# One unit forward: diagonals and first decays of the mLSTM heads, two value products behind a turn, and GpSimd's waits

## The chip, the cores and the metric

The kernel runs on one core of one Trainium2 chip. The metric is the device time of one execution in microseconds; lower is better. Everything is float32 at the interface. Large products are computed as three matmuls on operands split in a rounded part (fp32r, names ending in `_hi`) and a remainder (`_lo`).

## The reference

Two transformer blocks follow each other on a sequence of 512 tokens of width 1024. The first has a convolution branch, a sparse attention, a cross attention and a feed-forward layer. The change lies in the token mixer of the second block, which has two parts beside each other:

- an mLSTM of 4 heads (key width 64, value width 128): scores of queries and keys, weighted by a causal decay exp(gate of the key minus a running maximum m of the query), times the values; each row is divided by a norm, passed through an RMS norm, and gated;
- a latent causal attention (MLA) of 8 heads (q.k of width 96, value width 64) in query blocks of 128.

```
D = b[..., :, None] - b[..., None, :] + ig[..., None, :]
Dw = jnp.exp(D - m_comb[..., None])
s = jnp.einsum('bhcid,bhcjd->bhcij', qc, kc) * Dw
num = ... s @ v ...;  h = num / jnp.maximum(jnp.abs(den), jnp.exp(-m_comb))[..., None]
h_ml = rmsnorm(h_ml, ...) * jax.nn.sigmoid(o_ml)          # 4 heads
h_mla = causal_block_attention(q, k, kv[..., MLA_NOPE:])  # 8 heads, blocks of 128 queries
return jnp.concatenate([h_ml, h_mla], axis=-1) @ w_out
```

The kernel computes an mLSTM head without chunks: 4 key blocks jb of 128 keys, each against all queries from its own block on.

## The kernel before, in words

The program is one in-order list of instructions for each engine, written out by hand; semaphores join them. In the stretch that the change touches, every engine runs a loop over **units** n = 0 to 31, one for each of 8 latent heads x 4 query blocks, and then five more units (32 to 36). Unit n on TensorE (PE) is: the latent scores of unit n + 2, then a hook with the work of other stages (`beside`: steps of three 512-column matmuls of the mLSTM values and output gates, `BESIDE` says how many in each unit; `ml_turn`: the transposes of a finished mLSTM head; `ml_score`), then `ml_values` (the values of one key block), and at some units `latent_values(h)`, 10 matmuls (20 records) of a latent head whose probabilities went through HBM to be turned (`l_turned`).

mLSTM head h starts at unit 3 + 7h; its step st is n - 3 - 7h. By step:

- st -1, ACT (L2059 to L2064): DMA that broadcasts the head's row of m from HBM to all partitions (`mrow`);
- st 1, VectorE (DVE, L3114 to L3121): the four **diagonals** `negm_diag`, 128x128 each, from `mrow` and a mask. They wait for `mrow` and for the decays of the head before;
- st 2 to 5, ACT (L2066 to L2076): `decay` of key block 0 to 3, an exp of the diagonal block and one of the columns right of it. The one of block 0 is the **first decay**;
- st 3 to 6, PE: score of key block jb into the one bank `ps[3]`; DVE then multiplies it with the decay to `sT` (L3093), which frees the bank for the next score;
- st 4 to 7, PE: values of the block; the first of a head waits for `ml_gated`, that is for `hml` (L3137) of the head before, which takes its turned rows from the bank;
- st 7 and 8: squares on ACT (L2080), `ml_var` on DVE (L3110), the **root** on ACT (L2085). The root is a Sqrt, so ACT loads a table before it and another one before the next exp;
- st 9, DVE: `ml_rows` (L3124 to L3127), the scaled rows; st 11 (10 for the last head): `ml_turn` on PE (L1367), `hml` on DVE; st 12: `mix_hi` on ACT (L2088).

DVE's unit n is: reciprocal of the row sums n (`rowinv`, L3192), mask of unit n + 2 (L3186), `hml` where due, `sT`, the transpose of the probabilities of unit n - 1 (`l_parts`, L3199), `latent_lo`, then `ml_rest` with the diagonals or `ml_rows`. ACT's unit n is: `latent_hi`, probabilities n scaled by `rowinv` (L2135), exp of unit n + 2 (L2129), then its hook: weight casts (`cast_at`), the step of every head, output gates.

`latent_values(h)` needs the landed `l_turned`, and `latent_lo(h - 1)` on DVE, behind `latent_hi(h - 1)` on ACT, which empty its bank. SP issues, in an order written out by hand, the stores of `l_parts`, the loads of `l_turned` and the weight chunks `w_raw`. GpSimd (POOL) computes weight remainders `w_lo` (L655), `mix_lo` of the mLSTM heads (L726) and 16 products on the residual (L716, L719); waits place them.

Of the kernel before, what the change touches and what calls it, by code (L numbers as in the profile page):

```python
# [31 lines left out]
TB = T // P  # L32
# [10 lines left out]
ML_HEADS = 4  # L43
# [178 lines left out]
GATES_AT = 1  # L222
LATE_CASTS = 17


def turned_at(h):
    return 10 + (h < ML_HEADS - 1)


# [11 lines left out]
def program(nc, stream, xT, memT, cols_in, consts_in, pos_in, out):  # L241
    with ExitStack() as ctx:
# [406 lines left out]
        def _(pool):  # L649
# [72 lines left out]
            def ml_lo(h):  # L722
                pool.wait_ge(sems["ml_hi"], h + 1)
                if h == 1:
# [5 lines left out]
                              26: (14, 15)}  # L730
            def behind_diagonals(heads):
                pool.wait_ge(sems["ml_diag"], TB * heads)

            remainder(CH["OM"], CH["OM"] % RING)
            behind_diagonals(2)
            remainder(CH["OM"] + 1, (CH["OM"] + 1) % RING)
            for unit in (15, 16):
                second_residual(unit, residual_steps[unit])
            pool.wait_ge(sems["qk_silu"], 6)
            for unit in (17, 18):  # L740
                second_residual(unit, residual_steps[unit])
            behind_diagonals(3)
            remainder(CH["OM"] + 2, (CH["OM"] + 2) % RING)
            ml_lo(0)
            remainder(CH["WO"], 0)
            remainder(CH["WO"] + 1, 1)
            for unit in (23, 24, 25, 26):
                second_residual(unit, residual_steps[unit])
            behind_diagonals(4)
            ml_lo(1)  # L750
            remainder(CH["WO"] + 2, 2)
            ml_lo(2)
            pool.wait_ge(sems["ml_var"], ML_HEADS)
            remainder(CH["WO"] + 3, 3)
# [38 lines left out]
        def _(pe):  # L793
# [626 lines left out]
            for n in range(4 * MLA_HEADS):  # L1420
                if n + 2 < 4 * MLA_HEADS:
                    latent_scores(n + 2)
                turned = n == ML_START + ML_EVERY + turned_at(1)
                ml_hook(n)
                if not turned:
                    ml_values(n)
                if n % 4 == 1 and n >= 9:
                    latent_values(n // 4 - 2)
                if turned:
                    ml_values(n)  # L1430
                ml_turns(n)
# [163 lines left out]
        def _(act):  # L1595
# [461 lines left out]
            def ml_step(h, st):  # L2057
                if st == -1:
# [5 lines left out]
                    act.dma_start(mrow[:, :], m_rows[h:h + 1, :].to_broadcast([P, T])).then_inc(sems["ml_mrow"], 16)  # L2064
                if 2 <= st < 2 + TB:
                    jb = st - 2  # L2066
                    u = 4 * h + jb
                    act.wait_ge(sems["ml_diag"], TB * (h + 1))
                    if u >= 2:
                        act.wait_ge(sems["ml_sT"], u - 1)  # L2070
                    g = gcols[:, 0, jb, h:h + 1]
                    m = A.activation(decay[:, u % 2, 0:P], negm_diag[:, jb, :], ACT.Exp, bias=g)
                    if jb < TB - 1:
                        m = A.activation(decay[:, u % 2, P:T - jb * P], mrow[:, (jb + 1) * P:T], ACT.Exp,
                                         bias=g, scale=-1.0)
                    m.then_inc(sems["ml_decay"], 1)  # L2076
# [16 lines left out]
            def ml_hook(n):  # L2093
# [6 lines left out]
                if n in cast_at and n < LATE_CASTS:  # L2100
                    round_to(cast_at[n])
                for h in range(ML_HEADS):
                    ml_step(h, n - ML_START - ML_EVERY * h)
# [44 lines left out]
            for n in range(4 * MLA_HEADS):  # L2148
                if n % 4 == 2 and n >= 10:
                    latent_hi(n // 4 - 2)  # L2150
                latent_scaled(n)
# [135 lines left out]
        def _(dve):  # L2287
# [825 lines left out]
            def ml_step(h, st):  # L3113
                if st == 1:  # L3114
                    dve.wait_ge(sems["ml_mrow"], 16 * (h + 1))
# [102 lines left out]
            for n in range(4 * MLA_HEADS):  # L3218
# [5 lines left out]
                if n >= 1:  # L3224
                    latent_turn(n - 1)
                if n % 4 == 2 and n >= 10:
                    latent_lo(n // 4 - 2)
                ml_rest(n)
# [370 lines left out]
```

## Time and profile before

| | us |
|---|---|
| median of 3 runs | 1511.98 (1511.72 to 1512.5) |
| the profiled execution | 1512.39 |
| its span, first to last instruction | 1510.6 |
| PE busy | 1490.2 (99%) |
| DVE busy | 1128.3 (75%) |
| ACT busy | 751.5 (50%) |
| GpSimd busy | 627.2 (42%) |

The mean granted TensorE clock is 0.999. Shares of busy time are means over the whole program. Matmuls are pipelined: a 512-column fp32r matmul has 0.39 us in the trace, while the next one starts 0.23 us after it. A wait of PE shows in full in the distance from start to start, and only in part as idle time. The stretch of the units lies between about 1020 and 1135 us of the span.

### The profile page before, as it was taken

How to read it: one execution, taken by the hardware profiler on the slowest of the kernel's cores; microseconds unless marked ns; L12 is line 12 of the kernel's file. 1: busy time of each engine (PE TensorE's matmuls, PEld its weight loads, DVE VectorE, ACT ScalarE, POOL GpSimd, SP SyncE). 2: the span in 40 equal slices, each digit the busy share in tenths (PEclk: the TensorE clock that was granted, in tenths of full speed). 3: DMA queues.
4: the chain of work that ended last, by engine and by line, in shares of the span. 5: the costliest groups of instructions: out<-in, count | busy, mean ns of one | idle time of the engine just before them, and what ended most of it. 6: DMA issues, size and time to landing. Idle time of an engine off the chain costs nothing.

```text
span 1510.6 us, 20173 instructions
## 1 busy us (share of the span) xinstructions
PE 1490.2 (99%) x6978; PEld 1230.5 (81%) x6978; DVE 1128.3 (75%) x1872; ACT 751.5 (50%) x1255; POOL 627.2 (42%) x280
## 2 busy tenths in 40 slices
PE   9999999999999999999999999999999999999998
PEld 7888888878888887888888888786778888888887
DVE  5689999897875445776776768789755887777776
ACT  6553333454562345754544345464964745444434
POOL 3455444332334432144444445451544344444451
PEclk9999999999999999999999999999999999999999
DMA  5332333255543323323333123232653433333451
GB/s 212 98 126 98 98 95 95 89 158 156 158 156 98 98 83 112 102 94 98 112 98 107 54 84 98 84 98 88 181 151 106 144 114 92 109 121 114 142 136 56
DMA packets 77026, 170.40 MB, mean 113 GB/s; under 512 B 22660, under 2 KB 39172, under 8 KB 76680
## 3 DMA queue, kind: packets, MB, share of 16 engines
q1 hardware_dynamic: 75920, 165.64, 35.3%
q10 hardware_dynamic: 1016, 3.61, 0.7%
q8 instruction: 51, 0.84, 0.2%
q14 instruction: 39, 0.32, 0.1%
HBM read 154.54 MB, written 14.69 MB: 112 GB/s over the span
## 4 chain that ended last, share of the span: by engine, by line
PE 86%; DVE 4%; ACT 4%; issue 3%; POOL 1%; DMA 1%; SPq 0%; DVEq 0%; ACTq 0%; POOLq 0%
PE bank L795 86%; POOL w_lo L655 1%; DMA w_raw<-in_stream 1%; ACT w_hi L1604 1%; DVE x_sq L2359 0%; ACT l_probs L2129 0%; DVE bias L2441 0%; POOL res L764 0%; ACT l_probs L2135 0%; ACT dn_first L1898 0%; DVE qk_ml L2999 0%; DMA dn_raw<-in_stream 0%; PE bank L1214 0%; DVE res_tok L3420 0%; PE bank L905 0%
## 5 line engine op out<-in xcount | busy, mean ns | idle before, releaser
L655 POOL TENSOR_TENSOR w_lo<-w_raw,w_hi 128x1024 fp32r<-128x1024 f32 x191 | 472.5, 2484 | 519.2 <-ACT w_hi L1604 511.4
L795 PE MATMUL bank<-a_hi,w_hi 128*128 128x512 f32 (+1 forms) x1120 | 444.6, 397 | 1.8 <-DVE a_lo L3283 1.6
L795 PE MATMUL bank<-a_hi,w_lo 128*128 128x512 f32 (+1 forms) x1120 | 431.4, 385 | 0.0
L795 PE MATMUL bank<-a_lo,w_hi 128*128 128x512 f32 (+1 forms) x1120 | 431.2, 385 | 0.0
L1604 ACT CAST w_hi<-w_raw 128x1024 fp32r<-128x1024 f32 x199 | 204.6, 1046 | 174.2 <-DMA w_raw<-in_stream 174.1
L795 PEld LDWEIGHTS bank<-a_hi,w_hi 128*128 128x128 f32 x1120 | 210.5, 188 | 48.6 <-issue 3.9
L795 PEld LDWEIGHTS bank<-a_lo,w_hi 128*128 128x128 f32 x1120 | 210.5, 188 | 45.3 <-issue 3.4
L795 PEld LDWEIGHTS bank<-a_hi,w_lo 128*128 128x128 f32 x1120 | 210.4, 188 | 42.5
L667 POOL TENSOR_TENSOR dn_rest<-dn_raw,dn_second 128x1024 fp32r<-128x1024 f32 x39 | 93.7, 2433 | 248.3 <-DVE dn_rest L2734 248.3
L795 PE MATMUL bank<-dn_rest,f_hi 128*128 128x512 f32 x364 | 141.6, 389 | 0.0
L1898 ACT CAST dn_first<-dn_raw 128x1024 fp32r<-128x1024 f32 x54 | 55.6, 1049 | 157.8 <-DVE dn_raw L2715 157.8
L2793 DVE TENSOR_TENSOR ytok<-bank,ytok 128x512 f32<-128x512 f32 x88 | 59.6, 688 | 39.1 <-PE bank L795 38.7
L2505 DVE SCALAR_TENSOR_TENSOR bank<-conv_in,cols,bank 128x512 f32<-128x512 f32 x114 | 82.2, 751 | 1.6
L795 PE MATMUL bank<-dn_first,f_hi 128*128 128x512 f32 x208 | 81.4, 391 | 0.3 <-POOL dn_rest L667 0.3
L795 PE MATMUL bank<-dn_first,f_lo 128*128 128x512 f32 x208 | 81.0, 389 | 0.0
L795 PEld LDWEIGHTS bank<-dn_rest,f_hi 128*128 128x128 f32 x364 | 68.3, 188 | 14.0
L2484 DVE SCALAR_TENSOR_TENSOR bank<-conv_in,cols,bank 128x512 f32<-128x512 f32 x116 | 76.6, 747 | 0.0
L795 PE MATMUL bank<-b_hi,w_hi 128*128 128x512 f32 x160 | 64.1, 401 | 0.0
L795 PE MATMUL bank<-b_hi,w_lo 128*128 128x512 f32 x160 | 62.3, 390 | 0.0
L795 PE MATMUL bank<-b_lo,w_hi 128*128 128x512 f32 x160 | 62.3, 389 | 0.0
L2734 DVE TENSOR_TENSOR dn_rest<-dn_raw,dn_first 128x1024 fp32r<-128x1024 f32 x50 | 60.9, 1219 | 1.4 <-ACT dn_first L1898 1.3
L795 PE MATMUL bank<-dn_second,f_hi 128*128 128x512 f32 x156 | 61.0, 391 | 0.6 <-DVE ytok L2793 0.5
(428 smaller groups left out, 2763.0 us busy)
## 6 DMA issues: line engine op xcount, KB each, us to landing
w_raw<-in_stream SPq DMA_DIRECT2D x199, 512.0 KB, 3.5
dn_raw<-in_stream SPq DMA_DIRECT2D x56, 512.0 KB, 3.5
p_parts<-d_parts SPq DMA_DIRECT2D x8, 640.0 KB, 3.9
d_turned<-p_parts SPq DMA_DIRECT2D x32, 160.0 KB, 3.3
l_turned<-p_parts SPq DMA_DIRECT2D x32, 160.0 KB, 3.0
p_parts<-l_parts SPq DMA_DIRECT2D x8, 384.0 KB, 3.4
res<-in_xT ACTq DMA_DIRECT2D x1, 2048.0 KB, 7.8
p_parts<-l_parts SPq DMA_DIRECT2D x8, 256.0 KB, 2.4
```

The source lines that it names most:

```text
L655: nc.gpsimd.tensor_tensor(w_lo[:, j, :], w_raw[:, j, :], w_hi[:, j, :].bitcast(F32), ALU.subtract).then_inc(w_lo_done, 1)
L667: nc.gpsimd.tensor_tensor(dn_rest[:, n, :], dn_raw[:, n, :], dn_top[n].bitcast(F32), ALU.subtract).then_inc(sems["apart_lo"], 1)
L795: return nc.tensor.matmul(o, l, r, start=start, stop=stop)
L1604: A.copy(w_hi[:, slot, :], w_raw[:, slot, :]).then_inc(w_hi_done, 1)
L1898: A.copy(dn_top[n], dn_raw[:, n, :]).then_inc(sems["apart_hi"], 1)
L2484: V.scalar_tensor_tensor(out=blk(conv_io, e, 0, T) if last else acc, in0=u, scalar=w, in1=acc, op0=ALU.mult, op1=ALU.add).then_inc(sems["c ...
L2505: m = V.scalar_tensor_tensor(out=out, in0=u, scalar=w, in1=acc if start is None else start, op0=ALU.mult, op1=ALU.add)
L2734: V.tensor_tensor(dn_rest[:, n, :], dn_raw[:, n, :], dn_top[n].bitcast(F32), ALU.subtract).then_inc(sems["apart_lo"], 1)
L2793: V.tensor_tensor(dst[h], bank, dst[h], ALU.add).then_inc(sems["dn_evac"], 1)
```

## The change

The diagonals of heads 1 to 3 and their first decays come one unit earlier (head 0 keeps its place). In ACT's hook the heads are gone through from the last to the first, so where the first decay of head h and the root of head h - 1 fall in one unit, the decay now stands ahead of the root. `latent_values(1)` moves from unit 13 to 14 and `latent_values(5)` from 29 to 28, and in units 14, 21 and 28 (before in 21 alone) the latent values stand ahead of `ml_values`. `latent_hi(1)` and `latent_lo(1)` move from unit 14 to 15. GpSimd's waits for diagonals and for the silus become waits for `ml_var`; the residual products of units 23 and 24 come one wait earlier than the other four.

```diff
+VALUES_AT = {9: 0, 14: 1, 17: 2, 21: 3, 25: 4, 28: 5}
+SPLIT_AT = {10: 0, 15: 1, 18: 2, 22: 3, 26: 4, 30: 5}
+def diagonal_at(h):
+    return 1 - (h > 0)
...
-            def behind_diagonals(heads):
-                pool.wait_ge(sems["ml_diag"], TB * heads)
+            def behind_roots(heads):
+                pool.wait_ge(sems["ml_var"], heads)
             remainder(CH["OM"], CH["OM"] % RING)
-            behind_diagonals(2)
+            behind_roots(1)
             remainder(CH["OM"] + 1, (CH["OM"] + 1) % RING)
             for unit in (15, 16):
                 second_residual(unit, residual_steps[unit])
-            pool.wait_ge(sems["qk_silu"], 6)
+            behind_roots(2)
             for unit in (17, 18):
                 second_residual(unit, residual_steps[unit])
-            behind_diagonals(3)
             remainder(CH["OM"] + 2, (CH["OM"] + 2) % RING)
             ml_lo(0)
             remainder(CH["WO"], 0)
             remainder(CH["WO"] + 1, 1)
-            for unit in (23, 24, 25, 26):
+            for unit in (23, 24):
+                second_residual(22, residual_steps[unit])
+            behind_roots(3)
+            for unit in (25, 26):
                 second_residual(unit, residual_steps[unit])
-            behind_diagonals(4)
             ml_lo(1)
             remainder(CH["WO"] + 2, 2)
             ml_lo(2)
-            pool.wait_ge(sems["ml_var"], ML_HEADS)
+            behind_roots(ML_HEADS)
...
-                turned = n == ML_START + ML_EVERY + turned_at(1)
+                turned = n in [ML_START + ML_EVERY * h + turned_at(h) for h in range(ML_HEADS - 1)]
...
-                if n % 4 == 1 and n >= 9:
-                    latent_values(n // 4 - 2)
+                if n in VALUES_AT:
+                    latent_values(VALUES_AT[n])
...
-                if 2 <= st < 2 + TB:
-                    jb = st - 2
+                if 2 < st < 2 + TB or st == diagonal_at(h) + 1:
+                    jb = max(st - 2, 0)
...
-                for h in range(ML_HEADS):
+                for h in reversed(range(ML_HEADS)):
                     ml_step(h, n - ML_START - ML_EVERY * h)
...
-                if n % 4 == 2 and n >= 10:
-                    latent_hi(n // 4 - 2)
+                if n in SPLIT_AT:
+                    latent_hi(SPLIT_AT[n])
...
-                if st == 1:
+                if st == diagonal_at(h):
                     dve.wait_ge(sems["ml_mrow"], 16 * (h + 1))
...
-                if n % 4 == 2 and n >= 10:
-                    latent_lo(n // 4 - 2)
+                if n in SPLIT_AT:
+                    latent_lo(SPLIT_AT[n])
```

## Rows read from the trace of the kernel before

**Rows 1.** The page, part 1: busy time, share, instructions of each engine.

```profile
PE 1490.2 (99%) x6978; PEld 1230.5 (81%) x6978; DVE 1128.3 (75%) x1872; ACT 751.5 (50%) x1255; POOL 627.2 (42%) x280
```

**Rows 2.** A window of 10 us: busy time of PE, PEld, DVE, ACT, POOL.

```profile
1065.00:1075.00 10.00, 9.77 (x61) 7.92 (x59) 8.79 (x27) 9.87 (x22) 6.37 (x5) 1.00 0.59 171
```

**Rows 3.** Timeline of PE, head 1: start, length, [idle before, releaser].

```profile
1066.57 2.39 PE L795 MATMUL bank<-l_turned,v_mla 128*128 128x128 f32 x20
...
1069.72 0.60 PE L1367 MATMUL bank<-consts,ml_rows 128*128 128x128 f32 x4
1070.16 0.81 PE L795 MATMUL bank<-q_ml,qk_ml 128*128 128x384 f32 x2
1071.20 1.13 PE L795 MATMUL bank<-v_ml,sT 128*128 128x129 f32 x8 [0.23 <-DVE hml L3137]
```

**Rows 4.** Timeline of PE, head 2.

```profile
1087.57 0.60 PE L1367 MATMUL bank<-consts,ml_rows 128*128 128x128 f32 x4
1089.48 0.91 PE L795 MATMUL bank<-q_ml,qk_ml 128*128 128x384 f32 x2 [1.31 <-DVE sT L3093]
```

**Rows 5.** Timeline of PE, head 3.

```profile
1107.46 0.66 PE L1367 MATMUL bank<-consts,ml_rows 128*128 128x128 f32 x4
1109.36 0.91 PE L795 MATMUL bank<-q_ml,qk_ml 128*128 128x384 f32 x2 [1.24 <-DVE sT L3093]
1111.05 1.13 PE L795 MATMUL bank<-v_ml,sT 128*128 128x129 f32 x8 [0.78 <-DVE hml L3137]
1112.01 1.02 PE L795 MATMUL bank<-kh,qh 128*128 128x512 f32 x2
1112.87 0.59 PE L795 MATMUL bank<-q_ml,qk_ml 128*128 128x256 f32 x2
```

**Rows 6.** Timeline of ACT: root of head 0, first decay of head 1.

```profile
1064.31 0.20 ACT L2085 ACTIVATE mcol<-mcol 128x4 f32<-128x4 f32 x1
...
1067.63 0.40 ACT L2072 ACTIVATE decay<-negm_diag,gcols 128x128 f32<-128x128 f32 x1
...
1068.44 0.50 ACT L2135 ACTIVATE l_probs<-l_probs,rowinv 128x256 f32<-128x256 f32 x1
```

**Rows 7.** Timeline of DVE: diagonals of head 1, reciprocal of head 0, first sT.

```profile
1063.33 0.85 DVE L3119 SCALAR_TENSOR_TENSOR negm_diag<-mrow,consts 128x128 f32<-128x128 f32 x4
...
1065.27 0.13 DVE L3124 RECIPROCAL mcol<-mcol 128x4 f32<-128x4 f32 x1
...
1068.63 0.69 DVE L3093 SCALAR_TENSOR_TENSOR sT<-bank,decay 128x512 f32<-128x512 f32 x1
```

**Rows 8.** Timeline of ACT: root of head 1, first decay of head 2.

```profile
1085.16 0.21 ACT L2085 ACTIVATE mcol<-mcol 128x4 f32<-128x4 f32 x1
...
1087.75 0.39 ACT L2072 ACTIVATE decay<-negm_diag,gcols 128x128 f32<-128x128 f32 x1
```

**Rows 9.** Timeline of DVE: reciprocal of head 1, first sT of head 2.

```profile
1085.39 0.18 DVE L3124 RECIPROCAL mcol<-mcol 128x4 f32<-128x4 f32 x1
...
1088.73 0.69 DVE L3093 SCALAR_TENSOR_TENSOR sT<-bank,decay 128x512 f32<-128x512 f32 x1 [1.41 <-issue]
```

**Rows 10.** The line of the mrow DMA, head 3 alone: issue, and time to landing.

```profile
L2064 ACTq DMA_DIRECT2D mrow<-m_rows x1: 327/327/327, 1097.9 to 1097.9; - x1
...
DMA to landing us min/median/max: 4.2/4.2/4.2
```

**Rows 11.** The same line over the whole span: four DMAs, time to landing.

```profile
DMA to landing us min/median/max: 3.2/3.5/4.2
```

**Rows 12.** Timeline of DVE, unit 25.

```profile
1101.16 0.70 DVE L3186 CUSTOM_DVE_ANT_0 bank<-bank,consts 128x512 f32<-128x512 f32 x1 [1.23 <-PE bank L795]
```

**Rows 13.** Timeline of ACT: the table load ahead of the root of head 2.

```profile
1103.47 1.28 ACT L2085 ACT_TABLE_LOAD   x1
```

**Rows 14.** Timeline of SP: the load of latent head 5's turned probabilities.

```profile
1105.70 1.73 SPq L536 DMA_DIRECT2D l_turned<-p_parts  x4
```

**Rows 15.** The page, part 6: DMA issues, KB each, us to landing.

```profile
l_turned<-p_parts SPq DMA_DIRECT2D x32, 160.0 KB, 3.0
```

## The prediction

> **What bounds the kernel now.** I read the page first: PE is busy for 1490.2 of 1510.6 us [rows 1], so all that any edit off PE can give is the time in which PE waits. Then PE's waits in the stretch of the units, and then the timelines of the four engines there, side by side. Idle time of PE undercounts a wait, because the modelled end of a matmul hides its first 0.2 us; I take distances from start to start. Four transposes of 128 columns take 0.44 us from start to start [rows 3], so 384 columns of the same kind take about 0.33. With that, the waits around the three moved heads are:
> - head 1: the first values could start at 1070.16 + 0.33 = 1070.49 and start at 1071.20, 0.71 us late, behind `hml` [rows 3];
> - head 2: the second score could start at 1087.57 + 0.44 = 1088.01 and starts at 1089.48, 1.47 us late, behind the first `sT` [rows 4];
> - head 3: the second score 1109.36 - 1107.90 = 1.46 us late behind `sT`, the first values 1111.05 - 1109.69 = 1.36 late behind `hml`, the third score 1112.87 - 1112.45 = 0.42 late [rows 5].
>
> That is 5.4 us, 0.36% of the time, and it is the most that the edits can bring. What ends these waits is read from the other engines. ACT is busy for 9.87 of 10 us in the window of head 1 [rows 2]: it isn't the engine with the most work of the span, but here it hardly rests, and its first decay of head 2 ends the wait of `sT`: DVE had been idle for 1.41 us before that `sT` at 1088.73, right after the decay that began at 1087.75 [rows 8, 9]. What is moved ahead on ACT moves something else back by the same time.
>
> **The change part by part.** No instruction is added or removed on PE, ACT, DVE or SP; all prices are orders.
>
> *Decay ahead of the root.* The first decay takes 1068.44 - 1067.63 = 0.81 us [rows 6]. It leaves its place behind the root, the two table loads and one exp, and stands ahead of the root: the decay comes some 3 to 4 us earlier, the root 0.81 later. Table loads stay at two a head, since a decay beside exps needs none. What hangs on the root is the reciprocal and `ml_rows` on DVE, and behind these, in order on the same engine, the next mask and the first `sT`: the very one whose decay was hurried. So the wait for the decay becomes a wait for the root.
>
> *Diagonals one unit earlier.* Four of them take about 0.8 us of DVE [rows 7]. The work is the same, but now it stands ahead of the reciprocal, mask and `ml_var` of the next unit. Where DVE was waiting for PE anyway this is free; at head 1 it was not (ACT scaled the probabilities of unit 11 directly on the reciprocal that now comes 0.75 later). At heads 2 and 3 there is idle time of DVE to hold it: 1.23 us before the mask at 1101.16 [rows 12]. But there the diagonals need `mrow`.
>
> *Head 1.* The root was done by 1064.43 and the reciprocal started at 1065.27 [rows 6, 7]: 0.8 us of slack. The root moves back by 0.81 (decay) + 0.75 (diagonals ahead) = 1.56, so the reciprocal comes about 0.8 later. `ml_rows`, two memsets, a mask and then `sT` follow without a gap: `sT` was ready to start at 1068.4 but for the decay, starts now at about 1069.2, and frees the bank at about 1069.9. PE's second score starts there (before 1070.16, [rows 3]). Before, `latent_values(1)` lay in front of it and covered this wait; now it lies behind: 0.33 + 2.23 us (2.39 less its 0.16 tail, [rows 3]) and the first values start at 1069.95 + 2.56 = 1072.5 instead of 1071.20. Head 1 costs **+1.3 us**; its own wait of 0.71 is gone in that sum. Bounds: -0.7 if `sT` is free when PE comes (PE would be there at 1067.9), +2.2 if memsets and silus behind it slip too.
>
> *Head 2.* The shift of 1.3 is carried by PE, DVE and ACT. The root ends at 1085.27 + 1.3 + 0.81 = 1087.4; from the reciprocal (1085.39) to the moment DVE was free for `sT` (1088.73 - 1.41 = 1087.32) are 1.93 us, `sT` takes 0.61 to the next start [rows 9]: bank free at 1090.0. PE's second score starts at 1090.05 instead of 1089.48 [rows 4]. The balance after head 2 is **+0.6 us**: of the wait of 1.47, some 0.7 are won, against 1.3 brought along.
>
> *Head 3.* `mrow` was issued at 1097.9 and landed 4.2 us later, at 1102.1 [rows 10]; before, the diagonals came at 1103.5 and never waited. Now DVE reaches them at about 1099.9 (1101.16 - 1.23, [rows 12]) and stands, with the shift of 0.6, until 1102.7, and 0.8 more for the diagonals: the mask of unit 27's scores comes at 1103.5 instead of 1101.16 [rows 12]. What is queued behind it: its exp on ACT (0.8), then the decay (0.81), the table load and root (1.4 from 1103.47, [rows 13]) at 1107.3; on DVE `latent_lo` (0.6 behind `latent_hi` 0.5), `ml_rows` 1.2, so the turn at 1109.7 instead of 1107.46; mask, gate and `sT` 1.6 more, so the second score at 1111.35 instead of 1109.36 [rows 5]. Here the moved values pay: `latent_values(5)` (2.23) then runs while `hml` is made, and the first values start at 1111.35 + 0.33 + 2.23 = 1113.9; they take 0.96, so scores 31 start at 1114.9. Before they started at 1112.01, with 2.23 of latent values still to come, equal to 1114.24 now; and the 0.42 wait behind them is gone. Balance at the end of head 3: 0.66 - 0.42, **+0.3 us** rounded. The transfer for head 5 is issued from 1105.70 to 1107.43 [rows 14]; with 3.0 us for each [rows 15] it has landed by 1110.5 to 1111.3, just in time for PE at 1111.7.
>
> By the Trainium skill (DMA: Bandwidth & Descriptors, Anatomy of one DMA) a transfer costs about 2.0 us plus its bytes over 436 GB/s, 2.6 us for the 256 KB of `mrow` (its figure is one for GpSimd's queue; this one is ACT's). The trace has 4.2 for this one [rows 10], so the measurement decides; by the page's price the diagonals would wait 1.6 us less and head 3 would be won.
>
> *GpSimd.* Its waits for the diagonals become waits for `ml_var`, about 0.8 us earlier for head 0 and the same unit otherwise. Two pairs of residual products leave the silus for the second root, and two pairs leave the block of eight for a place behind the third root. This makes remainders up to 4 us later; their readers on PE are units 22 and 32 on, several us after that, and this cover hides it. I cost it at 0; if the cover were gone, PE would stand for up to as long as a remainder is late beyond it, which I bound by 2 us, and I see no gain in it for PE.
>
> *Sum.* +1.3 - 0.7 - 0.3 = +0.3 us. The profiled execution would go from 1512.39 to 1512.7; against the median of 1511.98 the same shift gives **1512.3 us**.
>
> **The rivals.**
> - *The waits go.* The root isn't late (or DVE's chain behind it shorter), `mrow` lands in about 3 us, and both waits for `sT`, that for `hml` and the last one go: 1.47 + 1.46 + 1.36 + 0.42 = 4.7 us, 1507.3. For it: each edit aims at one of these waits, and DVE has idle time. Against it: ACT has none, and the root stands where the decay stood. Half of it (2.3 us, 1509.7) is still no change by my bound.
> - *`mrow` decides.* The diagonals are moved against a DMA that is not moved. At head 3 the wait is 2 us; at head 2 it is 1.0 by my estimate (the median landing, 3.5 us [rows 11], against some 2.5 between issue and diagonals). If each such wait, and head 1's 1.3, goes through to PE in full, it is 1.3 + 1.0 + 2.5 (the mask's 2.3 and the shift) = 4.8: 1516.8, slower. It decides from a landing at head 3 later than about 1101.2 us, where DVE was idle anyway. Against it: `latent_values(5)` covers part.
> - *The cover fails at head 5.* PE comes before the turned probabilities have landed and stands for up to 1 us: 1513.3. This is within no change.
>
> **How the numbers follow.** What a measurement of this kernel can tell from no change is about 0.2%, 3.0 us. My forecast, the waits change places, gets 0.74 together with the third rival, its own range 1510.3 to 1513.8. The waits go beyond 3.0 us: 0.17. `mrow` decides beyond 3.0 us: 0.09. So faster 0.17, same 0.74, slower 0.09. The range that leaves out no more than 2 in 10 reaches into both: 1508.6 to 1514.4.
>
> **What would show it.** In the profile after: the first decay of head 2 about 3 us earlier and ahead of its root; the first `sT` of heads 1 and 2 right behind a mask, with no wait for a decay; a new idle time of PE of about 2 us before the second score of head 1, put down to `sT`, or hidden in part by the modelled ends; an idle time of DVE before the diagonals of head 3, ended by the `mrow` DMA; the wait for `hml` at head 3 gone. I am wrong if PE's second score of head 1 does not wait, if the mask of unit 27 comes before 1102.5 us, or if PE's start on w_out moves by more than 1.5 us either way.

## The result, and the profile after

The changed kernel takes 1516.96 us (median of 14 runs, 1513.66 to 1520.76), the kernel before beside it 1512.96 us (14 runs). The ratio is 1.0026, 95% interval 1.0018 to 1.0034: slower by 4.0 us, where 1512.3 was forecast with a range up to 1514.4.

The profiled execution of after took 1513.77 us with a span of 1512.0, one of the quickest of its runs. First the page, part 1 (busy time, share, instructions), for [rows 1]:

```profile
PE 1491.5 (99%) x6978; PEld 1230.4 (81%) x6978; DVE 1127.1 (75%) x1872; ACT 752.0 (50%) x1255; POOL 626.2 (41%) x280
```

No engine has more work, so the loss is in waits, or in the clock. Next PE's timeline (start, length, [idle before, releaser]), heads 1, 2 and 3 one behind the other, for [rows 3 to 5]. The first row of after, and the last, bound the **stretch**: from the first latent values to the last turn.

```profile
1055.70 2.40 PE L802 MATMUL bank<-l_turned,v_mla 128*128 128x128 f32 x20
...
1068.83 0.91 PE L802 MATMUL bank<-q_ml,qk_ml 128*128 128x384 f32 x2 [1.86 <-DVE sT L3100]
1069.58 2.39 PE L802 MATMUL bank<-l_turned,v_mla 128*128 128x128 f32 x20
1071.81 1.06 PE L802 MATMUL bank<-v_ml,sT 128*128 128x129 f32 x8
...
1089.60 0.91 PE L802 MATMUL bank<-q_ml,qk_ml 128*128 128x384 f32 x2 [0.48 <-DVE sT L3100]
...
1109.03 0.65 PE L1374 MATMUL bank<-consts,ml_rows 128*128 128x128 f32 x4 [1.31 <-DVE ml_rows L3134]
1110.63 0.91 PE L802 MATMUL bank<-q_ml,qk_ml 128*128 128x384 f32 x2 [0.94 <-DVE sT L3100]
1111.38 2.39 PE L802 MATMUL bank<-l_turned,v_mla 128*128 128x128 f32 x20
1113.61 1.06 PE L802 MATMUL bank<-v_ml,sT 128*128 128x129 f32 x8
1114.51 1.02 PE L802 MATMUL bank<-kh,qh 128*128 128x512 f32 x2
1115.37 0.59 PE L802 MATMUL bank<-q_ml,qk_ml 128*128 128x256 f32 x2
...
1117.86 0.49 PE L802 MATMUL bank<-v_ml,sT 128*128 128x129 f32 x2 [0.27 <-DVE sT L3100]
1118.11 0.48 PE L802 MATMUL bank<-mix_hi,w_hi 128*128 128x512 f32 x1
...
1124.86 0.66 PE L1374 MATMUL bank<-consts,ml_rows 128*128 128x128 f32 x4
```

The waits of before for `sT` at heads 2 and 3 are smaller (0.48 for 1.31, 0.94 for 1.24), that for `hml` at head 3 is gone, and two new ones stand in their place, before head 1's second score (1.86) and head 3's turn (1.31). The same two ends in the kernel before, and between them its latent values of head 5, the score behind them and its start on w_out:

```profile
1056.93 2.40 PE L795 MATMUL bank<-l_turned,v_mla 128*128 128x128 f32 x20
...
1113.97 2.40 PE L795 MATMUL bank<-l_turned,v_mla 128*128 128x128 f32 x20
1116.21 0.39 PE L795 MATMUL bank<-q_ml,qk_ml 128*128 128x128 f32 x2
...
1117.22 0.48 PE L795 MATMUL bank<-mix_hi,w_hi 128*128 128x512 f32 x1
...
1123.64 0.60 PE L1367 MATMUL bank<-consts,ml_rows 128*128 128x128 f32 x4
```

The stretch has grown from 66.71 to 69.16 us, +2.45. After enters it 1.23 us earlier, which doesn't follow the edits (over the profiles of the 16 executions here the entry lies anywhere between 1055.40 and 1058.03), so **1.23 is to be added to after's times** when they are set beside before's, as is done below.

DVE's timeline, for [rows 7, 9, 12]: reciprocals, diagonals, and the mask of unit 27.

```profile
1064.92 0.18 DVE L3131 RECIPROCAL mcol<-mcol 128x4 f32<-128x4 f32 x1 [0.81 <-ACT mcol L2092]
...
1068.10 0.68 DVE L3100 SCALAR_TENSOR_TENSOR sT<-bank,decay 128x512 f32<-128x512 f32 x1
...
1081.60 0.90 DVE L3126 SCALAR_TENSOR_TENSOR negm_diag<-mrow,consts 128x128 f32<-128x128 f32 x4 [0.81 <-DMA mrow<-m_rows]
...
1087.07 0.18 DVE L3131 RECIPROCAL mcol<-mcol 128x4 f32<-128x4 f32 x1 [1.61 <-ACT mcol L2092]
...
1101.79 0.90 DVE L3126 SCALAR_TENSOR_TENSOR negm_diag<-mrow,consts 128x128 f32<-128x128 f32 x4 [1.77 <-DMA mrow<-m_rows]
...
1102.68 0.68 DVE L3193 CUSTOM_DVE_ANT_0 bank<-bank,consts 128x512 f32<-128x512 f32 x1
```

ACT's timeline at head 2 (decay, now ahead of the root), for [rows 8]:

```profile
1084.61 0.41 ACT L2079 ACTIVATE decay<-negm_diag,gcols 128x128 f32<-128x128 f32 x1
1084.90 0.62 ACT L2081 ACTIVATE decay<-mrow,gcols 128x384 f32<-128x384 f32 x1
1085.54 1.28 ACT L2092 ACT_TABLE_LOAD   x1
1086.84 0.21 ACT L2092 ACTIVATE mcol<-mcol 128x4 f32<-128x4 f32 x1
```

And the line of the `mrow` DMA at head 3, for [rows 10]:

```profile
L2071 ACTq DMA_DIRECT2D mrow<-m_rows x1: 326/326/326, 1098.0 to 1098.0; - x1
...
DMA to landing us min/median/max: 3.7/3.7/3.7
```

**The rest goes with the clock.** 2.45 us isn't 4.0. The mean granted clock of each execution splits after's runs: 5 with 0.999 or more, median 1514.46; 9 below it, median 1518.07. Of the kernel before, whose granted clocks are on record only beside the experiments, in the last set of runs 15 at 0.999 or more have 1511.88 and 11 below it 1513.99. So at full clock the loss is 1514.46 - 1511.88 = 2.6 us, close to the stretch's 2.45; below it, 1518.07 - 1513.99 = 4.1. The changed kernel is more often below (17 of its 23 executions, the second set included, against 40 of 93 of the kernel before in all sets), and its median falls there. This is a comparison of groups, not an experiment; the first experiment shows one place where the clock falls.

### The profile page after: what moved, and what is told of

Its sections match the earlier page's. It is cut to its first block and busy times, and to the rows that moved or that the text cites. A ratio compares the mean times of both kernels' runs of the same rounds, so it can differ in the third digit from the quotient of the medians.

```text
span 1512.0 us, 20173 instructions
## 1 busy us (share of the span) xinstructions
PE 1491.5 (99%) x6978; PEld 1230.4 (81%) x6978; DVE 1127.1 (75%) x1872; ACT 752.0 (50%) x1255; POOL 626.2 (41%) x280
```

## The experiments

Ratios are to the kernel before run beside it, with 95% intervals; "stretch" is that of the one profiled execution (66.7 for before, 69.2 for after, both with a granted clock of 1.00 all through it). In eight of the profiles below the granted clock falls to 0.50 somewhere in the stretch, for 3.4 or 6.8 us at a time. Work at half the clock takes twice as long, so half of that time is what the fall took; it is given as "the clock's part" of the stretch.

**The changed kernel again**, unedited, for a second profile.

> The changed kernel once more, beside the others. The measure for the stretch is L, the time from PE's first latent values (unit 9) to the turn of the last head (unit 34): 1123.64 - 1056.93 = 66.7 us before, 1124.86 - 1055.70 = 69.2 after. Theory A, the units: L is 69.2 again within 0.3, and the time is 2.5 us (0.16%) above before. Theory B, something beside the units (the clock, the start): L is 69.2 and the time is 4 us (0.26%) above before, with a granted clock below that of before.

1517.84 us, ratio 1.0035 (1.0021 to 1.0048), stretch 71.3, the clock's part 1.7, so 69.6 without it. PE's timeline at head 1, and windows of PE (busy, granted clock, DMA share, GB/s):

```profile
1069.60 0.91 PE L802 MATMUL bank<-q_ml,qk_ml 128*128 128x384 f32 x2 [1.86 <-DVE sT L3100]
1070.34 3.92 PE L802 MATMUL bank<-l_turned,v_mla 128*128 128x128 f32 x20
```

```profile
1069.00:1070.00 1.00, 0.41 (x1) 1.00 0.00 0
1070.00:1071.00 1.00, 1.00 (x8) 0.97 0.00 0
1071.00:1072.00 1.00, 1.00 (x7) 0.50 0.09 25
1072.00:1073.00 1.00, 1.00 (x7) 0.50 0.00 0
1073.00:1074.00 1.00, 1.00 (x6) 0.50 0.00 0
1074.00:1075.00 1.00, 1.00 (x10) 0.83 0.00 0
```

The same wait of 1.86 us as in the first profile, but here the clock is at 0.50 (1.2 of 2.4 GHz) right behind it for some 3.4 us, and the latent values take 3.92 instead of 2.39. A wait of after so costs its length, and in some executions about 1.7 us more (half of 3.4).

**GpSimd's part alone**: before, with all that the change does to GpSimd; two places of it:

```diff
-            behind_diagonals(2)
+            behind_roots(1)
...
-            for unit in (23, 24, 25, 26):
+            for unit in (23, 24):
+                second_residual(22, residual_steps[unit])
+            behind_roots(3)
+            for unit in (25, 26):
```

> The kernel before with the new order and waits of GpSimd alone. Theory A (GpSimd's place costs nothing): L 66.7 within 0.3, time within 0.1% of before. Rival: later remainders or its use of SBUF beside VectorE cost, L above 67.5 and 1 to 2 us more; that would be the part of the loss that the units do not explain.

1520.9 us, ratio 1.0051 (1.0035 to 1.0067): slower than the whole change. The stretch is 73.9, and two falls of the clock have 3.4 of it: 70.5 without them, 3.8 above before. DVE's diagonals of heads 2 and 3, and GpSimd's timeline there:

```profile
1083.12 3.41 DVE L3120 SCALAR_TENSOR_TENSOR negm_diag<-mrow,consts 128x128 f32<-128x128 f32 x4
...
1106.85 4.20 DVE L3120 SCALAR_TENSOR_TENSOR negm_diag<-mrow,consts 128x128 f32<-128x128 f32 x4
```

```profile
1082.18 4.20 POOL L716 TENSOR_TENSOR res<-res,cols 128x512 f32<-128x512 f32 x4 [8.43 <-DVE mcol L3111]
...
1105.77 5.13 POOL L719 TENSOR_TENSOR res<-res,rstd 128x512 f32<-128x512 f32 x4 [6.21 <-DVE mcol L3111]
```

Four diagonals that take 0.85 us alone [rows 7] take 3.41 and 4.20 beside GpSimd's residual products: both run over the same microseconds. PE then stands for `ml_rows` for 1.47 and 2.92 us, and each time the clock falls behind the waits. The Trainium skill (SBUF — State Buffer, section SBUF: two separate sides) says that VectorE and GpSimd share one port pair under an exclusive lock, and counts a VectorE instruction with two SBUF inputs among those that need it; these are such, and the trace agrees. So GpSimd's edit doesn't bring time; it keeps GpSimd out of the moved diagonals' way, and alone it puts it in the way of the old ones.

**All but GpSimd's part**: after, with before's waits on GpSimd.

> The changed kernel with GpSimd's order and waits of before. In the run with GpSimd's part alone the four diagonals of heads 2 and 3 took 3.4 and 4.2 us instead of 0.85, beside GpSimd's residual products. Theory A (VectorE instructions with two operands in SBUF stand while GpSimd works, so GpSimd's part is needed by the moved diagonals and harmful without them): here the diagonals of head 2, in unit 17, meet the residual products behind the silus and take 2 us or more, and L is above 70. Rival (the long diagonals came from something else): they take 0.85 to 0.9 and L is 69.2.

1520.48 us, ratio 1.005 (1.0037 to 1.0064), stretch 76.1, of which three falls of the clock have 5.1: 71.0 without them, 1.4 to 1.8 above the changed kernel with its GpSimd part. DVE and GpSimd at head 2:

```profile
1083.42 2.45 DVE L3125 SCALAR_TENSOR_TENSOR negm_diag<-mrow,consts 128x128 f32<-128x128 f32 x4 [0.57 <-DMA mrow<-m_rows]
```

```profile
1081.24 4.08 POOL L722 TENSOR_TENSOR res<-res,cols 128x512 f32<-128x512 f32 x4 [6.24 <-DVE qk_ml L3148]
```

The same collision from the other side; the two parts belong together. (The four of head 3 took 1.11.)

**Latent values 1 at their old place**, all else as changed, diagonals of head 1 early too.

```diff
-VALUES_AT = {9: 0, 14: 1, 17: 2, 21: 3, 25: 4, 28: 5}
-SPLIT_AT = {10: 0, 15: 1, 18: 2, 22: 3, 26: 4, 30: 5}
+VALUES_AT = {9: 0, 13: 1, 17: 2, 21: 3, 25: 4, 28: 5}
+SPLIT_AT = {10: 0, 14: 1, 18: 2, 22: 3, 26: 4, 30: 5}
...
-                turned = n in [ML_START + ML_EVERY * h + turned_at(h) for h in range(ML_HEADS - 1)]
+                turned = n in [ML_START + ML_EVERY * h + turned_at(h) for h in range(1, ML_HEADS - 1)]
```

> The changed kernel with the values of latent head 1 back in unit 13, in front of the second score of head 1 (and its split in unit 14). Theory A (head 1 loses because nothing covers the wait for the first sT any more): the wait of 1.9 us before PE's second score of head 1 is under 0.5, the first values of head 1 start 1.5 to 1.9 us earlier, and L is 67.5 to 68.2, as part is taken back by the root of head 1. Rival (the loss is made at heads 2 and 3 alone, by ACT): L stays at 69.

1514.67 us, ratio 1.0013 (1.0003 to 1.0024). The stretch is 69.4, the same as after's, but 1.7 of it is a fall of the clock at head 3: 67.7 without it, inside the 67.5 to 68.2 of the theory. At head 1 PE is as before, first values behind a mere 0.24 of `hml`:

```profile
1071.01 1.13 PE L802 MATMUL bank<-v_ml,sT 128*128 128x129 f32 x8 [0.24 <-DVE hml L3144]
...
1108.71 0.66 PE L1374 MATMUL bank<-consts,ml_rows 128*128 128x128 f32 x4 [1.29 <-DVE ml_rows L3134]
```

Half of the loss or more goes with this one edit, with the diagonals and the first decay of head 1 still early. The wait at head 3's turn (1.29) stays as in after (1.31).

**`mrow` issued earlier**, right behind the last decay of the head before.

```diff
-                if st == -1:
+                if st == -1 and h == 0:
...
+                if st == 5 and h < ML_HEADS - 1:
+                    act.wait_ge(sems["ml_diag"], TB * (h + 1))
+                    act.wait_ge(sems["ml_decay"], TB * (h + 1))
+                    act.dma_start(mrow[:, :], m_rows[h + 1:h + 2, :].to_broadcast([P, T])).then_inc(sems["ml_mrow"], 16)
```

> The changed kernel with the mrow DMA of heads 1 to 3 issued right behind the last decay of the head before, one unit earlier. Theory A (diagonals of head 3 wait for their DMA): VectorE's waits of 0.8 and 1.8 us before the diagonals of heads 2 and 3 go, the mask of unit 27 comes 1 to 1.5 us earlier, L is 67.7 to 68.4. Rival (the root behind the decay sets head 3, the landing is hidden): L 69.0 or more.

1517.59 us, ratio 1.0028 (1.0015 to 1.004). At head 2 the diagonals wait no more. At head 3 nothing is won: the whole stretch is later, the issue falls at 1100.84, 0.37 us ahead of a 512 KB weight chunk on SP's queue, and the 256 KB of `mrow` take 6.6 us to land; the diagonals wait 2.87. The stretch is 73.6, the clock's part 1.7, so 71.9 without it where 67.7 to 68.4 was expected; 1.74 of it is a new wait of PE for the turned probabilities of a latent head. The theory couldn't be tested in this way, because the landing moved with the issue.

**Root first**: ACT goes through the heads forward again, the decay one unit early.

```diff
-                for h in reversed(range(ML_HEADS)):
+                for h in range(ML_HEADS):
```

> The changed kernel with ACT's heads in the old order, so that the root of head h - 1 stands ahead of the first decay of head h in their unit. Theory A (the root pushed back by the decay sets the first sT, and with it PE's second score): the root comes 0.8 us earlier at each head, PE's wait before the second score of head 1 falls from 1.9 to about 1.1, that at the turn of head 3's unit from 1.3 to about 0.5, and L is 67.7 to 68.5. Rival (the decay is now late again, as it waits for a table load behind the root): the first sT of heads 1 and 2 waits for the decay and L stays at 69 or more.

1518.27 us, ratio 1.0038 (1.0024 to 1.0052). Head 1's wait falls from 1.86 to 1.18, that is 0.68 of the 0.81 that the forecast gives for a decay ahead of a root. The rest of that wait is no work of the order: in the kernel before, `sT` started at 1068.63 [rows 7], 0.7 us ahead of after's (1068.10 + 1.23 = 1069.33), and the latent values covered the time up to it. At head 3 the turn waits 3.29 us for `ml_rows`, with a fall of the clock of 6.8 us behind it. `mrow` landed after 4.3 us there and the diagonals waited 2.33, but the longer wait is ACT's: behind the root stand a second table load and the decay, `latent_hi` of latent head 4 comes behind these, and DVE waits for it:

```profile
1107.97 0.68 DVE L3214 TENSOR_TENSOR mix_lo<-bank,mix_hi 64x512 fp32r<-64x512 f32 x1 [3.49 <-ACT mix_hi L2148]
```

The stretch is 72.8, the clock's part 3.4: 69.4 without it, no shorter than after's. So the order explains less than half of head 1's wait, and the total is no better, as the rival had it.

**Head 0's turn five times**, to fill PE's wait at head 1 with idle transposes (four extra rounds of the same four; the result is unchanged).

```diff
-                for qb in range(TB):
-                    m = nc.tensor.transpose(ps[0][:, qb * P:(qb + 1) * P], ml_rows[:, qb, :], ident)
+                for again in range(5 if h == 0 else 1):
+                    for qb in range(TB):
+                        m = nc.tensor.transpose(ps[0][:, qb * P:(qb + 1) * P], ml_rows[:, qb, :], ident)
```

> The changed kernel; PE makes the four transposes of the turn of mLSTM head 0 five times over instead of once (the same result), which puts 1.8 us of work in its idle time before the second score of head 1. Theory A (the long idle time there makes the TensorE clock fall in most executions, and that is what the medians lose beyond the 2.5 us of the traced execution): no fall of the granted clock around 1070 us, L 69.2 or a few tenths more, the runs closer together and their median 1514 to 1516, 1 to 3 us below the changed kernel's 1517.8. Rival (the spread comes from elsewhere, or the clock falls at other places as well): median 1517 or more, the profile with a fall of the clock, L above 70.5.

1516.6 us, ratio 1.0034 (1.0021 to 1.0048); clock 1.0 in the profile, stretch 70.0. Without the fall the stretch is 1.3 us shorter than that of the unedited kernel with it (71.3), and 0.8 longer than that of the unedited kernel without it (69.2); the wait at head 3's turn was 2.01 here against 1.31. Of its five runs two still have a clock below 0.999 (median 1520.17; the three others 1516.52), and the median of all, 1516.6, lies between the theory's 1516 and the rival's 1517. Inconclusive for what the clock does to the median.

**Head 1 as before** (diagonals, first decay and latent values 1).

```diff
-    return 1 - (h > 0)
+    return 1 - (h > 1)
...
+VALUES_AT = {9: 0, 13: 1, 17: 2, 21: 3, 25: 4, 28: 5}
+SPLIT_AT = {10: 0, 14: 1, 18: 2, 22: 3, 26: 4, 30: 5}
...
-                turned = n in [ML_START + ML_EVERY * h + turned_at(h) for h in range(ML_HEADS - 1)]
+                turned = n in [ML_START + ML_EVERY * h + turned_at(h) for h in range(1, ML_HEADS - 1)]
```

> The changed kernel with head 1 as it was: its diagonals and first decay one unit later again, the values of latent head 1 in unit 13, its split in unit 14. Heads 2 and 3, the order on ACT and GpSimd stay changed. Theory A (head 1 is where the loss begins and ACT carries 0.8 us of it on; the rest is the wait for mrow at head 3): PE up to the first values of head 1 as before, L 67 to 68 without a fall of the clock (1.6 more with one). Rival (head 1 doesn't matter to the end of the stretch): L 69 or more without a fall.

1515.43 us, ratio 1.0015 (1.0006 to 1.0024); the 3 runs at full clock have 1512.95, the 8 others 1516.51. The ratio is no lower than with the latent values 1 alone moved back (1.0013), so what head 1 loses comes from the latent values behind its second score, and nothing that could be measured from its early diagonals and decay. And something else is left. The stretch is 72.7, the clock's part 3.4, so 69.3 without it: the theory's 67 to 68 was missed, and the number is the rival's. Its profile shows why. DVE's diagonals of head 3, PE's turn, and the line of `mrow`:

```profile
1103.27 0.90 DVE L3126 SCALAR_TENSOR_TENSOR negm_diag<-mrow,consts 128x128 f32<-128x128 f32 x4 [4.74 <-DMA mrow<-m_rows]
```

```profile
1110.50 1.12 PE L1374 MATMUL bank<-consts,ml_rows 128*128 128x128 f32 x4 [3.83 <-DVE ml_rows L3134]
1112.10 1.65 PE L802 MATMUL bank<-q_ml,qk_ml 128*128 128x384 f32 x2 [0.48 <-DVE sT L3100]
1113.54 4.17 PE L802 MATMUL bank<-l_turned,v_mla 128*128 128x128 f32 x20
```

```profile
L2071 ACTq DMA_DIRECT2D mrow<-m_rows x1: 327/327/327, 1096.5 to 1096.5; - x1
...
DMA to landing us min/median/max: 6.7/6.7/6.7
```

`mrow` was issued 1.5 us earlier than in after, and 0.25 us behind a 512 KB weight chunk (in after 3.2 behind it), took 6.7 us instead of 3.7, and the early diagonals hand the lateness on to the turn (a wait of 3.83 us). The clock's fall behind it lasts 6.8 us.

**Only head 3 as before**, and **heads 1 and 3 as before**. In both GpSimd waits for head 3's diagonals where the changed kernel has it wait for the third `ml_var`, so that nothing meets them. The second also has `VALUES_AT`, `SPLIT_AT` and `turned` of the kernel with head 1 as before. The two versions of one line stand below each other, with a remark behind each:

```diff
-    return 1 - (h > 0)
+    return 1 - (0 < h < ML_HEADS - 1)     # head 3 alone
+    return 1 - (h == 2)                   # heads 1 and 3, with VALUES_AT 13: 1
...
-            behind_roots(3)
+            pool.wait_ge(sems["ml_diag"], TB * 4)
```

> Open: how much of the loss is head 3's diagonals standing before the DMA of mrow. This is the changed kernel with the diagonals and the first decay of head 3 at their old place; GpSimd waits for head 3's diagonals where the changed kernel waits for the third root, so that its residual products don't meet the diagonals; heads 1 and 2, the moved latent values and the order of heads on ACT are as changed. Theory (the mrow wait of head 3 is a cause of its own, of 1.5 to 2.5 us with the clock's fall behind it): the diagonals of head 3 don't wait, the turn of head 3 waits for ml_rows under 0.5 us (1.31 to 3.3 in the kernels with the early diagonals), the first sT of head 3 waits again for its decay (about 1.2 us on PE), the stretch from the first latent values to the last turn is 67.5 to 69 us, and the median is 1514.5 to 1515.5, a ratio of 1.0015. Rival (the fall of the clock at head 1 is the whole loss, and head 3 only changes one wait for another): the stretch stays at 69 to 71 us and the ratio at 1.0025 to 1.0035.

> Only head 2 has its diagonals and first decay one unit early; heads 1 and 3 are at their old places, with GpSimd's wait for head 3 as in the kernel above; ACT goes through the heads from the last to the first, and latent values 5 come in unit 28, ahead of the mLSTM values, split(4) in 26 as before. Theory: with no early diagonals at head 3 the long waits seen there (3.83 and 2.33 us) can't come back, and no unit has an idle time of PE of 1.9 us; the stretch is 66.5 to 67.5 us, the clock doesn't fall, and the median is that of the kernel before within 0.05% (ratio 0.9995 to 1.0007). Rival (the remaining loss of the kernel with head 1 at its old place, 1.0015, comes from head 2 or from GpSimd's new waits, not from head 3): the ratio stays at 1.0012 to 1.002.

Head 3 alone: 1516.58 us, 1.0023 (1.0012 to 1.0034). Both: 1513.79 us, 1.0006 (0.9997 to 1.0015). In the first the wait before head 3's turn has shrunk to 0.39 as expected, but the expected 1.0015 was too low: its interval holds both that and the rival's 1.0025 to 1.0035. Its stretch, expected at 67.5 to 69, is 71.1, the clock's part 1.7: 69.4 without it, no shorter than the 69.2 and 69.6 of the changed kernel. In place of the wait for `mrow` stand one of 0.98 for `sT` and one of 0.91 for the turned probabilities of head 5. The second came out as its theory said, at the upper end, with a stretch of 66.6 and no fall. PE's timeline of the first shows another entry for the clock:

```profile
1109.72 0.66 PE L1374 MATMUL bank<-consts,ml_rows 128*128 128x128 f32 x4 [0.39 <-DVE ml_rows L3134]
1111.36 0.91 PE L802 MATMUL bank<-q_ml,qk_ml 128*128 128x384 f32 x2 [0.98 <-DVE sT L3100]
1113.18 4.13 PE L802 MATMUL bank<-l_turned,v_mla 128*128 128x128 f32 x20 [0.91 <-DMA l_turned<-p_parts]
```

Three waits of under 1 us each in 4 us, and the clock falls (4.13 for 2.39); in the same profile the 1.86 of head 1 did not make it fall. The four kernels together:

| ratio to before | head 3 early | head 3 as before |
|---|---|---|
| head 1 early | 1.0026, again 1.0035 | 1.0023 |
| head 1 early, latent values 1 at their old place | 1.0013 | not run |
| head 1 as before | 1.0015 | 1.0006 |

Head 1 is worth 0.0011 to 0.002 in the left column and 0.0017 in the right (1.7 to 3.0 us), head 3 0.0003 to 0.0012 in the upper row and 0.0009 in the lower (0.5 to 1.8 us). The intervals are about 0.001 wide to either side, so head 1's part is shown and head 3's is not: no pair of ratios that differ in head 3 alone is clear of noise, and the stretches without the clock's part differ by nothing in the upper row and by 2.7 (69.3 to 66.6) in the lower, where `mrow` took 6.7 us. With both undone, head 2 alone being early, no loss can be told from none.

**Latent values 5 alone**: before, with latent values 5 in unit 28, ahead of the mLSTM values.

> The kernel before with the values of latent head 5 in unit 28, ahead of the first values of mLSTM head 3, and nothing else. Theory A (they cover the wait for hml): the 0.8 us of idle time before the first values of head 3 go, the landing is just in time, and L is 65.8 to 66.3. Rival (the turned probabilities land too late): PE waits for their DMA and L is 66.7 or more.

1512.46 us, ratio 1.0001 (0.9992 to 1.001), stretch 67.1. The wait for `hml` at head 3 goes, and one of 0.79 for `sT` comes later: a wait changes place. PE doesn't wait for the landing, so the rival's number came without its cause.

**Decay one unit early behind the root, with latent values 5**; nothing moved on DVE's diagonals.

```diff
-                turned = n == ML_START + ML_EVERY + turned_at(1)
+                turned = n in (21, 28)
...
-                if 2 <= st < 2 + TB:
-                    jb = st - 2
+                if 2 < st < 2 + TB or st == (1 if h > 0 else 2):
+                    jb = max(st - 2, 0)
...
+VALUES_AT = {9: 0, 13: 1, 17: 2, 21: 3, 25: 4, 28: 5}
+SPLIT_AT = {10: 0, 14: 1, 18: 2, 22: 3, 27: 4, 30: 5}
```

> A try at a version better than both: the kernel before (diagonals, GpSimd, latent head 1 as they were), with the first decay of heads 1 to 3 right behind the root of the head before, in the same unit, the values of latent head 5 in unit 28 ahead of ml_values, and the split of head 4 in unit 27. Theory A (the wait for the first sT was one for the decay, and is won if the root is not pushed back): the first sT of head 2 starts 1 us or more earlier against PE's units, the waits of 1.3 and 1.2 us before the second scores of heads 2 and 3 fall to 0.5 or less, and L is 64 to 65.5. Rival (ACT is full, so the time comes back elsewhere, by exps that are late): L 66.5 or more.

1510.95 us, ratio 0.9991 (0.9982 to 1.0), stretch 65.8. Of the 2.55 us of waits for `sT` of heads 2 and 3 before, 0.24 and 0.52 are left:

```profile
1086.88 0.91 PE L797 MATMUL bank<-q_ml,qk_ml 128*128 128x384 f32 x2 [0.24 <-DVE sT L3095]
...
1105.95 0.91 PE L797 MATMUL bank<-q_ml,qk_ml 128*128 128x384 f32 x2 [0.52 <-DVE sT L3095]
```

**The same without latent values 5** (split 4 in unit 27 as there).

> The kernel before with the first decays of heads 1 to 3 right behind the root of the head before and the split of latent head 4 in unit 27, without the move of the values of latent head 5. Theory A (that move runs into the landing of the turned probabilities, 0.5 us of PE, and is worth little): L 65.4 to 66, time 1 to 2 us below before, the same as with the move or better. Rival (the move is what covers hml): L 66.4 or more.

1511.49 us, ratio 0.9995 (0.9986 to 1.0004), stretch 65.3.

**The better version again.**

> The version that beat the kernel before by 0.09% in one set of runs (the first decays of heads 1 to 3 behind the root before them in the same unit, latent values 5 in unit 28, split(4) in 27, nothing of diagonals or GpSimd moved), run again. Theory: it takes away 1.4 us of PE's waits and adds none of over 1 us, so the clock doesn't fall: stretch 65.5 to 66 us, ratio 0.9985 to 0.9995. Rival (the 0.09% was chance between runs): ratio 0.9997 to 1.0005.

1512.52 us, ratio 0.9997 (0.9987 to 1.0006), stretch 66.3. That is the ratio of the rival, and one thing in the theory failed outright: in this profile PE waits 1.21 us for the turned probabilities of latent head 5 (0.53 in the first). The mean of the two ratios is 0.9994. No interval lies clear of one, so a gain of about 1 us over the kernel before is possible, and not shown.

## Why the prediction was wrong

**Right.** Root and decay changed places and the wait with them: head 1's second score at 1068.83 + 1.23 = 1070.06, forecast 1069.95. The `mrow` wait of head 3: mask of unit 27 at 1102.68 + 1.23 = 1103.91, forecast 1103.5, in part by luck: `mrow` was issued at 1098.04 + 1.23 = 1099.3, 0.8 later than forecast, and landed in 3.7 instead of 4.2 us, and DVE stood for 1.77 of the 2.8 us that the forecast gives. The wait for `hml` is gone. The landing for head 5 came in time, in this profile; in four others with the same move PE waited 0.18 to 1.21 us for it.

**The step that failed in the sum: "four transposes of 128 columns take 0.44 us from start to start, so 384 columns of the same kind take about 0.33".** The row of a score [rows 3] is `x2`: two records of 384 columns, 768 in all, 0.66 by the same rate. After shows 0.75 for it (1068.83 to 1069.58, 1110.63 to 1111.38). By that the waits to be won were 0.29 + 1.47 + 1.46 + 0.94 = 4.2 us, not 5.4, and the last of them (0.42 before the third score) was none: from the 2 x 512 columns to it are 0.86 us in before (1112.01 to 1112.87, [rows 5]) and in after (1114.51 to 1115.37) alike. The balance, step by step:

- Head 1, forecast +1.3: first values at 1071.81 + 1.23 = 1073.04 against 1071.20, **+1.84**. 0.42 of the 0.54 missing is the second record.
- Head 2, forecast +0.6: second score at 1090.83 against 1089.48, **+1.35**. The 0.54 came in with head 1; the other 0.2 lies in ACT's and DVE's chain, where the reciprocal waits 1.61 for the root and the diagonals 0.81 for `mrow`, which this step of the forecast had left to the rival. That head 2 itself costs nothing is shown by the kernel with latent values 1 at their old place: there its second score is 1089.30 - 1056.72 = 32.58 us behind the entry, 32.55 in before and 33.90 in after.
- Head 3, forecast +0.3: w_out starts at 1118.11 + 1.23 = 1119.34 against 1117.22, **+2.12**, beyond the 1.5 that the forecast named as a sign of being wrong. 0.77 are lost where 0.3 was to be won. 0.42 is the second record ahead of the latent values and 0.42 the wait that was none. Another 0.63 is what the moved `latent_values(5)` had covered and the forecast left out: from the third score to w_out there are 2.74 us now (1115.37 to 1118.11), and 2.11 before without the latent values (1112.87 to 1117.22, less 1113.97 to 1116.21). Against these, some 0.3 were regained ahead of head 3's second score. Of the 0.33 that follow up to the last turn (2.45) the cause wasn't sought.

**The step that was missing: the clock.** The sum prices a wait of PE at its length, and a fall of the clock at nothing. The traces put 1.2 GHz behind some waits: for 3.4 us in the second profile of the changed kernel at head 1 and in the kernel with head 3 as before, behind three short waits; for 6.8 us in the kernel with head 1 as before and in the one with the root first, at head 3. Which execution it hits differs for the same wait: behind the 1.86 us at head 1 the clock fell in three profiles of five. By the split of the runs this takes the median from +2.6 at full clock to +4.0 us. That size is argued and not shown: the one experiment aimed at it, head 0's turn five times, had no fall in its profile and the same ratio (1.0034 for 1.0035). The Trainium skill (TensorE: Matmul & The Clock Gate, Part 1) says that a hardware monitor sets TensorE's clock to one half or to full by how busy it has been recently, and that the number of matmuls that one kernel runs at half the clock differs from run to run. The two profiles of the unedited kernel, one with the fall and one without, agree.

**GpSimd "at 0".** The edit carried a price of its own sign: left out, it costs 1.005 less the 1.0026 or 1.0035 of the whole change, 2.3 to 3.6 us, and alone it costs 0.0051, 7.7 us. In the one profile of each, falls of the clock have 5.1 us of the stretch in the first and 3.4 in the second. The forecast looked only at who reads GpSimd's results; what it does to DVE while it works it did not ask.

**The rival "`mrow` decides"** had 1516.8 us, 0.2 from what was measured, at 0.09. Its mechanism is there, in waits of DVE of 0.81 us at head 2 and 1.77 at head 3. But no ratio shows a price of it at head 3 clear of noise (0.5 to 1.8 us), and with head 2 alone early no loss can be told from none. Its head 1 term was in the forecast too, and the stretch of the profile grew by 2.45 us, not by its 4.8. That its time was right is luck. Against it I had set one profiled landing; over the eight profiles with early diagonals at head 3 it was 3.7, 4.3, 3.5, 3.7, 6.6, 4.3, 4.4 and 6.7 us.

## What to carry to other kernels

Read the count of a row before dividing its time, and check a "wait" worked out from distances against the idle time that the row gives. Where the bound engine is 99% busy, price a new wait not by its length alone but also by what the granted clock does behind it, and look for that in more than one profile: the same wait can have a fall behind it in one and none in another. Work that covers a wait uncovers it when it is moved: ask what stood behind it at its old place. A step that is moved in front of a DMA inherits the spread of its landing, and one that is moved beside another engine's work has to be looked at on both engines.

## What the hardware showed beside that

- At head 3 the broadcast of 256 KB took 6.7 and 6.6 us to land in the two profiles where it was issued within 0.4 us of a 512 KB chunk (the kernel with head 1 as before, and `mrow` issued earlier). In the 14 others it came 2.3 to 3.2 us behind one and took 3.5 to 5.5, and within them the distance doesn't order the landings (4.2 at 2.8 in before, 3.7 at 3.2 in after, 5.5 at 2.8 with only head 3 as before). Two profiles are no proof of the cause. By the formula of the Trainium skill (DMA: Bandwidth & Descriptors, Anatomy of one DMA), which is one for GpSimd's queue, the estimate would be 2.6 us; no profile here shows so little at head 3.
- Four 128x128 instructions of DVE with two SBUF inputs took 0.85 us alone and 4.20 us beside four of GpSimd.
- The clock was halved behind an idle time of 1.86 us of PE at head 1 in three profiles and not in two, once behind two of 1.29 and 0.94 us (latent values 1 at their old place), and once behind three of 0.39, 0.98 and 0.91 us. It stayed at half for 3.4 us, and for 6.8 us in the two profiles where PE had waited 3.29 and 3.83 us at head 3's turn.
